# A fused transformer kernel on one core: two norms folded into fewer passes, and the latents' norms moved between the state-space output products

## The reference

```python
# first block
z = layer_norm(x) @ w_in                       # xs, gs, cq (256), ckv (128), kr (64), gm
ys = s5_branch(xs, ...) * silu(gs)             # state-space scan, gelu, gated by a GLU
q = rms_norm(cq, q_norm_g) @ w_uq              # then rotary on a part
kv = rms_norm(ckv, kv_norm_g) @ w_ukv
ym = attention(q, k, v) * silu(gm)
u = ALPHA * x + concat([ys, ym]) @ w_out
x = layer_norm(u + sigmoid(u @ w_pg) * (p @ w_pp), ln_g, ln_b)            # ln_1
# second block; ada = silu(c) @ w_ada + b_ada gives shift, scale and gate, twice
h = rmsnorm(x, g_mix) * (1 + scale1) + shift1                             # rms_mix
x = x + gate1 * (merged_attentions(h @ w_in) @ w_out)
h2 = rmsnorm(x, g_ffn) * (1 + scale2) + shift2                            # rms_ffn
x = x + gate2 * (gelu(conv(h2 @ w_up)_gate) * conv(h2 @ w_up)_val) @ w_down
return rmsnorm(x, g_final)                                                # final
```

## Time and profile before

| | |
|---|---|
| median of 3 runs | 2528.74 us (2527.84 to 2532.51) |
| profiled execution, own time | 2508.37 us |
| its span | 2506.6 us |
| PE busy | 2302.1 us, 92% |
| DVE, ACT, POOL busy | 894.0, 567.1, 996.7 us |
| PE's share of the chain that ended last | 88% |
| mean granted clock of the PE | 0.955 of full speed |

### The profile page before, as it was taken

The page is one execution under the profiler, slowest core; times in us unless marked ns, Lnnn a source line. Parts: engine busy times, 40 slices in busy tenths (PEclk is TensorE's granted clock), DMA queues, the critical chain, the costliest instruction groups (busy, mean ns, idle before and its releaser), DMA issues.

```text
span 2506.6 us, 27327 instructions
## 1 busy us (share of the span) xinstructions
PE 2302.1 (92%) x11158; PEld 1682.6 (67%) x11158; DVE 894.0 (36%) x1257; ACT 567.1 (23%) x833; POOL 996.7 (40%) x658
## 2 busy tenths in 40 slices
PE   5999978898998499999998999997999999989995
PEld 1454443575876188557866888775888888868884
DVE  5940822442055501450046111145322333232334
ACT  3111122232011600561046000113111111111213
POOL 1533210203788057335655344332433344334441
PEclk8999978999999699999999999998999999999997
DMA  2326230001222122101211111122111111121111
GB/s 113 109 61 109 84 85 26 17 1 42 101 71 94 75 81 84 41 24 34 84 20 54 51 51 42 59 101 101 44 49 50 50 45 47 50 109 42 51 34 67
DMA packets 52439, 153.89 MB, mean 61 GB/s; under 512 B 13991, under 2 KB 16343, under 8 KB 52287
## 3 DMA queue, kind: packets, MB, share of 16 engines
q1 hardware_dynamic: 42720, 118.13, 14.2%
q10 hardware_dynamic: 6544, 23.87, 2.5%
q0 software_dynamic: 3072, 10.43, 2.2%
HBM read 133.37 MB, written 16.81 MB: 60 GB/s over the span
## 4 chain that ended last, share of the span: by engine, by line
PE 88%; DVE 5%; ACT 4%; DMA 2%; issue 1%; POOL 0%; ACTq 0%; DVEq 0%; SPq 0%; POOLq 0%
PE ps L1694 44%; PE ps L1652 12%; PE ps L2033 10%; PE ps L1932 4%; PE ps L1974 3%; PE ps L265 2%; PE ps L431 1%; PE ps L419 1%; PE ps L288 1%; PE ps L1772 1%; PE ps L556 1%; PE ps L568 1%; PE ps L545 1%; PE ps L413 1%; ACT back L748 1%
## 5 line engine op out<-in xcount | busy, mean ns | idle before, releaser
L1694 PE MATMUL ps<-h_high,w_parts 128*128 128x512 f32 x2688 | 732.5, 392 | 23.6 <-DVE h_low L1541 17.5
L1694 PEld LDWEIGHTS ps<-h_high,w_parts 128*128 128x128 f32 x2688 | 505.1, 189 | 129.6 <-issue 25.6
L980 POOL TENSOR_TENSOR w_parts<-front,sb_zero 128x1024 fp32r<-128x1024 f32 x138 | 267.1, 1936 | 791.1 <-PE ps L1694 467.5
L1694 PE MATMUL ps<-h_low,w_parts 128*128 128x512 f32 x1344 | 416.4, 391 | 0.0
L983 POOL TENSOR_TENSOR w_parts<-front,w_parts 128x1024 fp32r<-128x1024 f32 x138 | 349.9, 2536 | 10.9
L1694 PEld LDWEIGHTS ps<-h_low,w_parts 128*128 128x128 f32 x1344 | 253.9, 189 | 53.5
L2033 PE MATMUL ps<-ffn_parts,w_parts 128*128 128x512 f32 x1056 | 242.3, 392 | 10.7 <-DVE ffn_parts L1628 9.2
L2033 PEld LDWEIGHTS ps<-ffn_parts,w_parts 128*128 128x128 f32 x1056 | 199.8, 189 | 53.2 <-issue 11.5
L1652 PE MATMUL ps<-front 128*128 128x512 f32 x512 | 229.3, 606 | 6.1 <-DMA front<-w_in 3.4
L912 POOL TENSOR_TENSOR front<-front,sb_csilu 128x1024 f32<-128x1024 f32 x48 | 98.2, 2046 | 213.9 <-DMA front<-w_ada 198.6
L1652 PEld LDWEIGHTS ps<-front 128*128 128x128 f32 x512 | 97.7, 194 | 124.6 <-issue 119.9
(11 more groups left out here) (258 smaller groups left out, 2768.8 us busy)
## 6 DMA issues: line engine op xcount, KB each, us to landing
front<-w_ada SPq DMA_DIRECT2D x48, 512.0 KB, 3.5
front<-w_up SPq DMA_DIRECT2D x44, 512.0 KB, 3.4
front<-w_down SPq DMA_DIRECT2D x22, 512.0 KB, 3.4
front<-w_in SPq DMA_DIRECT2D x16, 512.0 KB, 3.5
front<-w_out SPq DMA_DIRECT2D x16, 512.0 KB, 3.6
residual<-back ACTq DMA_DIRECT2D x2, 4096.0 KB, 12.7
front<-w_gates SPq DMA_DIRECT2D x16, 512.0 KB, 3.4
front<-xT ACTq DMA_DIRECT2D x4, 1024.0 KB, 13.2
```

Of the source, the lines that this page charges most:

```text
L980: pool.tensor_tensor(parts[n % 2], raw, zero[:, 0:1].to_broadcast((P, PAGE)), ALU.add)\
L1694: mm = pe.matmul(ps[:, bank + nt, :], w_[:, k * P:(k + 1) * P], x_[k][:, nt * BANK:(nt + 1) * BANK], start=at == 0 and n == 0, stop=at == ...
```

## The change

**Latents.** The three tiles' squares, sums, roots and spreads are placed between the products x = 25 and x = 28. ACT squares tiles 0 and 1 before its copy of x = 24. The sums go to bank 7, the spreads to banks 0 to 3 (`LATENT`), the temporaries move to pages 45, 46 and half of 44. ACT no longer waits for `YF` before kv and q tiles: the wait for the y stores stands before the q copies, the one for `YF` before the gelu. POOL's kr and mask loads stand before the y stores. The second rotary tile goes to banks 4 to 7.

**ln_1 and rms_mix.** DVE scales `X2` by gain and rstd in one instruction. ACT squares with the bias `ln_b` added on the fly; the biased tile goes to `HV` (and from there to the spill, at the end). The spread of the second norm is copied to page 15, DVE multiplies `HV` with it, and ACT makes the rounded part and a full copy (`H4`, four pages in turn) from it with gain and shift. The table of biases by distance takes two products instead of four, three copies instead of six, and stands before the squares.

**rms_ffn.** The last square is summed by the PE and not added by DVE. ACT makes all high parts first from DVE's scaled tiles, and then the full tiles. The PE takes the high parts of the first two up tiles before their low parts (`up_first`).

**final.** Four squares are summed by the PE; DVE applies gain and rstd in one instruction, and SP stores when DVE is done.

```diff
         def sum_pe(pe, N, T):
-            pe.wait_ge(S("tile_added"), added_to(N, FT - 1))
-            sum_tiles(pe, 2, ones[:], T[2], True, True).then_inc(S("norm_square_used"), 1)
+            pe.wait_ge(S("tile_added"), added_to(N, ADDED[N] - 1))
+            if N == "final":
+                pe.wait_ge(S("x4_ready"), 5)
+            sum_tiles(pe, 0, ones[:], T[2], True, False)
+            for k in range(ADDED[N], FT):
+                pe.wait_ge(S("norm_square"), tiles_to(N, k + 1))
+                sum_tiles(pe, 0, ones[:], T[k % 2], False, k == FT - 1).then_inc(S("norm_square_used"), 1)
...
+        def latent_sums_pe(pe, i):
+            pe.wait_ge(S("norm_square"), tiles_to("kv_norm", i + 1))
+            ones_ = ones_q if i else ones_kv
+            sum_tiles(pe, 7, ones_[:], TEMPS_2[i % 2], i < 2, i != 1).then_inc(S("norm_square_used"), 1)
+
+        def latent_spread_pe(pe, N):
+            pe.wait_ge(S("norm_rstd"), norms_to(N))
...
+            for j in range(4):
+                at = slice(32 * j, 32 * j + 32)
+                mm = pe.matmul(ps[:, j, 0:256], pick[at, :], TEMPS_2[2][at, 256:512], start=True, stop=True)
+            mm.then_inc(S("norm_spread"), 1)
...
+            latent_square_act(act, 0)
+            latent_square_act(act, 1)
             for x in range(24, 32):
...
+                if x == 25:
+                    latent_root_act(act, "kv_norm", 0)
+                    latent_square_act(act, 2)
+                if x == 26:
+                    latent_gain_act(act, 0)
+                    latent_root_act(act, "q_norm", 2)
+                if x == 28:
+                    latent_gain_act(act, 1)
+                    latent_gain_act(act, 2)
...
-            act.wait_ge(S("yf_landed"), 16)
             for m in range(4):
                 act.wait_ge(S("kv_tile"), m + 1)
...
+            act.wait_ge(S("y_in_dram"), 16 * STEP)
             for m in range(4):
                 act.wait_ge(S("q_tile"), m + 1)
                 act.activation(QN[:, m, :], two(2 * (m % 2)), ACT.Copy).then_inc(S("q_free"), 1)
 
+            act.wait_ge(S("yf_landed"), 16)
...
+            act.activation(near[:, 191:320], ps[0:HEADS2, 1, 0:129], ACT.Copy).then_inc(S("dist_free"), 1)
+            act.activation(every4[:, 0:239], ps[0:HEADS2, 3, 0:239], ACT.Copy).then_inc(S("dist_free"), 1)
+            act.activation(every4[:, 272:512], ps[0:HEADS2, 3, 272:512], ACT.Copy).then_inc(S("dist_free"), 1)
...
+            biased(0)
+            act.wait_ge(S("norm_square_used"), tiles_to("rms_mix", FT))
+            act.activation(TEMPS_3[2][:, 256:512], ps[:, 2, 0:256], ACT.Sqrt, bias=eps[:, 1:2]).then_inc(S("norm_std"), 1)
+            act.wait_ge(S("gains_made"), 1)
+            for k in range(FT):
+                if k + 1 < FT:
+                    biased(k + 1)
+                act.wait_ge(S("norm_scaled"), tiles_to("rms_mix", k + 1))
+                act.activation(HH[k], X2[:, k, :], ACT.Identity, scale=gains[:, k:k + 1], bias=ada[:, k:k + 1])\
+                    .then_inc(S("norm_ready"), 1)
+                if k >= 4:
+                    act.wait_ge(S("h_split"), k - 3)
+                act.activation(H4[:, k % 4, :], X2[:, k, :], ACT.Identity, scale=gains[:, k:k + 1], bias=ada[:, k:k + 1])\
+                    .then_inc(S("h_high"), 1)
+            act.dma_start(x_spill, HV).then_inc(S("x2_spilled"), 16)
...
+            rstd_dve(dve, "ln_1", FT, lambda k: X2[:, k, :], True, TEMPS_3, modulation_1)
+            for k in range(FT):
+                x = quarters(X2[:, k, :])
+                dve.scalar_tensor_tensor(x, x, V("ln_g", k), SPREAD, ALU.mult, ALU.mult).then_inc(S("norm_scaled"), 1)
+            rstd_dve(dve, "rms_mix", FT, None, False, TEMPS_3)
+            dve.tensor_copy(quarters(page(15)), SPREAD).then_inc(S("norm_stat_read"), 1)
...
+            for k in range(FT):
+                dve.wait_ge(S("norm_ready"), y_ready(k))
+                dve.tensor_tensor(X2[:, k, :], HV[:, k, :], page(15), ALU.mult).then_inc(S("norm_scaled"), 1)
+                if k:
+                    low_mix(k - 1)
+            low_mix(FT - 1)
...
+            rstd_dve(dve, "final", FT, None, False, TEMPS_4)
+            for k in range(FT):
+                x = quarters(X4[:, k, :])
+                dve.scalar_tensor_tensor(x, x, V("g_final", k), SPREAD, ALU.mult, ALU.mult).then_inc(S("norm_ready"), 1)
...
+                if x == 25:
+                    latent_sums_pe(pe, 0)
+                if x == 26:
+                    latent_spread_pe(pe, "kv_norm")
+                    latent_sums_pe(pe, 1)
+                    latent_sums_pe(pe, 2)
+                if x == 28:
+                    latent_spread_pe(pe, "q_norm")
...
+                tile(4 * m, (B_UQ + 1) % RING, lambda k: CQ[:, k, :], kts=2, at=m * P, step=BANK)
+                tile(4 * m + 2, (B_UQ + 1) % RING, lambda k: CQ[:, k, :], kts=2, at=(2 + m) * P, step=BANK)\
                     .then_inc(S("qr_tile"), 1)
...
+            def up_first():
+
+                for late in (False, True):
+                    for m in range(2):
+                        n = nth(B_UP + m)
+                        pe.wait_ge(S("w_split"), n + 1)
+                        for k in range(FT):
+                            pe.wait_ge(S("h_split" if late else "h_high"), 3 * FT + k + 1)
+                            for w_ in (0,) if late else (0, 2):
...
+                                    if late and m and k == 0 and nt == 0:
+                                        mm.then_inc(S("w_used"), 1)
+                        if late:
+                            mm.then_inc(S("up_tile"), 1)
```

More of the change, by code:

```diff
@@ L740, in norm_act @@
                 .then_inc(S("norm_std"), 1)
+        def norm_act(act, N, kts, src, dst, gain, bias, epscol, centered, T):
+            squares_act(act, N, kts, src, epscol, centered, T)
             for k in range(kts):
                 act.wait_ge(S("norm_scaled"), tiles_to(N, k + 1))
-                if then and k > 0:
-                    then(k - 1)
                 if bias is None:
@@ L768, in program, with latent_dve @@
+        def latent_dve(dve, N, tiles):
+            dve.wait_ge(S("norm_std"), norms_to(N))
+            dve.reciprocal(TEMPS_2[2][:, 256:512], TEMPS_2[2][:, 256:512]).then_inc(S("norm_rstd"), 1)
+            dve.wait_ge(S("norm_spread"), norms_to(N))
+            for i in tiles:
+                x = quarters(latent(i)[0])
+                dve.tensor_tensor(x, x, LATENT, ALU.mult).then_inc(S("norm_scaled"), 1)
         TEMPS_1 = (page(24), page(25), page(26))
-        TEMPS_2 = (page(44), page(45), page(46))
+        TEMPS_2 = (page(45), page(46), cols(44 * PAGE + 512, 45 * PAGE))
@@ L2010, in up_body @@
                             pe.wait_ge(S("up_taps"), i * 4 + (2 * j + half - 3))
-                        start = first and j == 0 and half == 0
-                        tile3(4 * j + 2 * half, n % 2, None if start else "w_used", 3 * FT if start else None)\
-                            .then_inc(S("up_tile"), 1)
+                        tile3(4 * j + 2 * half, n % 2, "w_used").then_inc(S("up_tile"), 1)
             up_body(0)
```

206 lines of the change are left out of this document (115 added, 91 removed).

## The result

| | before | after |
|---|---|---|
| median | 2528.34 us (4 runs, 2527.84 to 2532.51) | 2433.16 us (4 runs, 2431.38 to 2435.93) |
| ratio, 95% interval | | 0.9621 (0.9604 to 0.9638) |
| profiled execution, own time | 2508.37 us | 2434.49 us |
| its span | 2506.6 us | 2432.7 us |
| mean granted clock in it | 0.955 | 0.975 |

Between the two profiled executions the gain is 2506.6 − 2432.7 = 73.9 us, where the sum of the terms said 73.0. So the miss is not in the terms. It is in the 20.4 us between the profiled execution of before and its runs: the four runs of after don't have them.

What follows compares the result with a forecast made beforehand. Long products were taken as PE-bound, with gains only where the PE waits around the norms. Terms 37.0 + 21.3 + 10.1 + 4.6 = 73.0 us gave 2435.4 profiled, 2455.7 us as median; range 2443 to 2475.

Steps and rivals of the forecast that it cites:

- A: Latents: norms done among the products and y's wait moved let kv tiles start at once; gain 37.0 us.
- B: ln_1 and rms_mix: serial elementwise work shortened, so the first values product starts earlier; gain 21.3 us.
- C: rms_ffn: last square summed on the PE, up tiles started early on high parts; gain 10.1 us.
- D: Final norm: adds of last squares removed, gains folded into DVE's scaling pass; gain 4.6 us.
- The y stores come late: Latents: POOL's loads ahead delay the y stores, holding the third q tile 19.3 us; 2475.0 us, chance 0.08.
- Half clock in the piecemeal pass: rms_ffn: up's 64 high-part records run at half clock, 13.1 us more; 2468.8 us, chance 0.05.
- Slower through the clock in the long products: Long products: less idling brings a lower clock; at 4% lower, 19 us slower, 2548 us, chance 0.02.
- The norms are not waited for: All four norms: another wait ends last in each place, under 5 us gained; 2526 us, chance 0.02.

Runs made afterwards that it cites:

- b1: The kernel before, unchanged, run again: short runs' median 2505.1 us, 7 of 10 runs long at 2527.6 to 2530.6 us.
- a1: The changed kernel again, only a comment line added: 2430.4, 2431.0, 2431.8, 2442.5, 2460.9 and 2464.9 us.
- e1: The kernel before with only the latents' part of the change: short runs' median 2468.0 us, 1 of 4 long at 2497.3 us.
- e2: The changed kernel with the latents' part undone: short runs' median 2470.7 us, 1 of 5 long at 2493.5 us.
- e7: The changed kernel with ACT's wait for `YF` back ahead of the kv copies: four runs 2456.0 to 2457.2 us, one 2485.9 us.
- e8: Changed kernel without the seam (last modulation column's one-column matmuls and TensorE's wait ahead of product 24): five runs 2430.8 to 2435.2 us, a sixth 7236.15.
- e9: The kernel before with one-column matmuls moved inside tile 15 and TensorE's wait behind product 24: 12 runs, 2500.1 to 2511.3 us, none long.
- e10: The kernel before with sixteen unread full matmuls between the one-column matmuls with their wait and product 24: 12 runs, 2517.6 to 2524.4 us, none long.
- e5: The kernel before with one unread full matmul behind each product 24 to 31: five of twelve runs 2540.6 to 2544.8 us, five 2510.5 to 2512.8, two between.
- e4: The kernel before with five groups of unread sums among the products: 8 runs 2506.6 to 2513.9 us, 4 runs 2517.7 to 2520.0 us.
- e6: The changed kernel with up's first tiles in the old order: 2442.5, 2443.1, 2443.8 and 2450.8 us.

## Why the prediction was right or wrong

**The step that failed** is the one sentence "The median of the three runs shown is 2528.74, 20.4 us longer; I carry that difference over unchanged." The 20.4 us are no constant that lies around a profiled execution. They belong to the two ways of running, 23 to 34 us apart by kernel: in the long one TensorE makes the products 24 to 31 at half clock (54.00 us at 0.50 in b1). All runs of before that were shown were long and its profiled execution short, and the runs of after came out short. Against the short way of before the forecast was right: 2508.37 − 73.0 = 2435.4, measured 2434.49 and a median of 2433.16. What I had added to it was after's long way, and that exists: 2460.9 and 2464.9 in a1, 5 us and more above the forecast. The profile and the runs that lay before me already differed by 0.8%, with the runs among themselves within 0.2%, and the range took in only 7 of these 20 us downwards. With the upper end of the terms it had to reach 2508.4 − 78.6 = 2429.8.

**The terms**, by the shift of one point between the profiled executions:

| point | before | after | shift | since the last | forecast |
|---|---|---|---|---|---|
| last sigmoid of GLU | 451.73 | 414.27 | 37.5 | A 37.5 | 37.0 |
| ln_1's spread | 822.70 | 784.31 | 38.4 | 0.9 | 0 |
| first values product | 868.48 | 809.58 | 58.9 | B 20.5 | 21.3 |
| last read of wo2 | 1722.74 | 1663.59 | 59.2 | 0.3 | 0 |
| third up tile | 1767.1 | 1698.75 | 68.3 | C 9.2 | 10.1 |
| end of down's last reads | 2482.07 | 2413.27 | 68.8 | 0.5 | 0 |
| end | 2506.6 | 2432.7 | 73.9 | D 5.1 | 4.6 |

That the sum is met within 0.9 us is in part luck: A and D gave 1.0 more, B and C 1.7 less, and 1.7 came between the terms, where the forecast had nothing.

- *A.* 74.7 us from the products to the sigmoid (forecast "some 75"), the PE busy 0.93 of it. The added work in the products was taken too dear: a spread on a busy PE took 0.71 us, near the lower of my two ends (0.64 and 1.28), and from product 24's start to the kv products (303.77 to 340.49) it is 36.7 us, 2.8 more than the 33.9 before (303.42 to 337.3), and I had 4.0.
- *B.* 0.8 less. ACT's squares start 3.7 us behind the spread's end (785.59 to 789.32; I had 3.4), and the eight take 9.4 us, not 9.0: with the bias in them 1.14 each, and the sum of the tile before, at half clock, now and then in their way. DVE's instruction with the gain took 1.27 by its line and 1.22 in the chain (forecast 1.22).
- *C.* 0.9 less. (The third up tile of before starts at 1767.1 by the order of the records from 1743.65; the prediction had 1767.3.) The first up tiles start on a PE that had idled: the granted clock is 0.91 from 1673 to 1699. The pass over the high parts takes 16.49 us (forecast 16.1), but not in the way that was forecast: the PE was to wait for each part, and it never does (busy 16.48 us, below). In its first 4 us, at a clock of 0.51, it falls behind ACT, and then always finds a part ready. The 64 records need 14.6 us at 0.228 each; half clock added 1.9 where the forecast had 1.5 of waiting, so the term came out right there by luck. The wait of the third tile for POOL is 1.24 us (forecast 1.1).
- *D.* 0.5 more. A part of it is DVE's pass: six scales take 7.15 us, 1.19 each, and not the 1.21 that I had.

**The rivals.** *The y stores come late*: they were issued at 341.4, as soon as the last copy allowed, each landed within 11.3 us, and the four q tiles ran as one block of 32 records without a gap (356.53, 13.99 us). *Half clock in the piecemeal pass*: only its start was. Busy time by stretch of after, the pass over the high parts and its first 4 us (columns as in the first such view):

```profile
1673.60:1690.09 16.49, 16.48 (x64) 13.44 (x65) 14.03 (x13) 16.49 (x15) 0.00 (x0) 0.88 0.28 112
1673.60:1677.60 4.00, 3.99 (x10) 3.14 (x11) 4.00 (x4) 4.00 (x4) 0.00 (x0) 0.51 1.02 420
```

The rule of the Trainium skill, page "TensorE: Matmul & The Clock Gate", section "A second HAM failure mode: psum-queue depth-cycling", is about frequent short idles. There were none here, so this run says nothing for or against it, and the rival's condition never came about. *Slower through the clock in the long products*: 468.76 of 470.00 us at 1.00. But what spoke for this rival, the 20 us of the runs, was a matter of the clock after all, in another place: not in the long products, but in 54 us of small ones. *The norms are not waited for*: e1, e2 and e7 say that they are, with the wait for y.

**A version without the long way.** e8 is the changed kernel with the seam closed: five runs from 2430.8 to 2435.2, ratio to before 0.9691 (0.9651 to 0.9732), where a1 in its job had 0.9719 (0.9665 to 0.9773). The short way is the same. That e8 has no long one is too little to go by with five runs, and rests on e9 and e10.

## What to carry to other kernels

When the profiled execution and the runs differ by more than the runs do among themselves, the profile may show another way of running. Look for where the same work takes different times before adding anything to a sum, or let the range hold both. A wait and the work that hides behind it are one term: here 8 and 12 us apart, 37 together. And an engine's short pause ahead of a long stream of small matmuls can cost more than the pause. Here 25 us were lost in about one run of four with a seam of 0.6 us, in none of 17 without it, and closing it cost nothing.

## What the runs showed of the hardware

- The PE kept half clock for 54 us of work without a gap (128x128 and 64x128 against 128 columns, fp32), in some executions of a program, and full clock through the same stream in others. What decides between them in one execution is not known.
- The clock fell at one place, 3.8 to 4.2 us behind the seam, in all seven profiles that lost it, and never later in the stream.
- One run of e8 (7236.15 us) had a mean granted clock of 0.316. Neither 0.50 nor 1.00, the two levels of all the profiles here, gives a mean so low, so the clock must have been lower still for a time; no profile was taken of it.
- Two full records to each 24 small ones did not bring the clock back in the profile of e5. In those of e4 and e6 it was back behind sums of 256 columns, in a1 only at the kv products.
- The unchanged program built a second time (b1) had 7 of 10 long runs and the kernel before 5 of 18 in the same job. Whether the share belongs to the copy or is chance (4% by the numbers) is open.
